# First gate computed by TensorE in units placed between attention's, with x modulated during the memory stage, more steps in each head, and the first feed-forward units split by K

## The reference, cut to what matters

```
mod = silu(c) @ w_ada + b_ada                 # one row of 2048 times 2048 x 12288
shift_m, scale_m, gate_m, shift_f, scale_f, gate_f = split(mod, 6)
h = rmsnorm(x) * (1 + scale_m) + shift_m
proj = h @ w_in                               # differential attention and MLA inputs
mix = concat(o_diff, o_mla) @ w_out
x = x + gate_m * mix
h = rmsnorm(x) * (1 + scale_f) + shift_f
x = x + gate_f * (relu(h @ w_ff1)**2 @ w_ff2)
# second block: memory keys and values from mem @ w_mem_kv, three attention branches,
# gates by sigmoid, output product
```

## Time and profile before

| | |
|---|---|
| median of 3 executions | 2192.8 us (2191.8 to 2196.15) |
| profiled execution, its own time | 2190.42 us |
| its span | 2188.6 us |
| mean granted TensorE clock | 0.961 of full speed |
| busy: PE, DVE, ACT, POOL | 2000.1, 1313.3, 945.3, 157.9 us |
| HBM read | 443 MB |

### The profile page before, as it was taken

The page is one execution under the profiler, slowest core; times in us unless marked ns, Lnnn a source line. Parts: engine busy times, 40 slices in busy tenths (PEclk is TensorE's granted clock), DMA queues, the critical chain, the costliest instruction groups (busy, mean ns, idle before and its releaser), DMA issues. The chain is left out here.

```text
span 2188.6 us, 24524 instructions
## 1 busy us (share of the span) xinstructions
PE 2000.1 (91%) x9240; PEld 1642.4 (75%) x9240; DVE 1313.3 (60%) x2057; ACT 945.3 (43%) x1440; POOL 157.9 (7%) x118
## 2 busy tenths in 40 slices
PE   6598897867789999999999999979999999999999
PEld 3276775546667888888888878878988877787877
DVE  3777876776796555555555555566555545545544
ACT  2453445343444344434434455445444444444433
POOL 0100000001000110110010021110100001101000
PEclk9798999878999999999999999989999999999999
DMA  9798775657797555555555555434534456656644
GB/s 356 284 327 307 244 250 199 235 189 278 290 340 255 192 192 184 192 193 186 188 193 187 187 193 179 149 100 126 164 108 149 126 169 198 192 182 187 194 170 170
DMA packets 128967, 448.82 MB, mean 205 GB/s; under 512 B 14288, under 2 KB 14544, under 8 KB 128336
## 3 DMA queue, kind: packets, MB, share of 16 engines
q1 hardware_dynamic: 124928, 433.74, 59.8%
q0 software_dynamic: 1568, 7.34, 0.9%
q10 hardware_dynamic: 2352, 6.17, 0.7%
HBM read 443.00 MB, written 4.19 MB: 204 GB/s over the span
## 5 line engine op out<-in xcount | busy, mean ns | idle before, releaser
L283 DVE TENSOR_TENSOR wlo<-raw,whi 128x1024 fp32r<-128x1024 f32 (+4 forms) x652 | 784.9, 1208 | 750.3 <-ACT whi L282 695.5
L282 ACT ACTIVATE whi<-raw 128x1024 fp32r<-128x1024 f32 (+4 forms) x652 | 658.3, 1012 | 836.6 <-PE g L397 707.0
L392 PE MATMUL g<-whi,lhsA_hi 128*128 128x512 f32 (+4 forms) x1840 | 715.8, 391 | 35.6 <-DVE lhsA_lo L788 28.0
L393 PE MATMUL g<-whi,lhsA_lo 128*128 128x512 f32 (+4 forms) x1840 | 698.0, 381 | 0.0
L397 PE MATMUL g<-wlo,lhsA_hi 128*128 128x512 f32 (+4 forms) x1840 | 470.0, 378 | 0.2 <-DVE wlo L283 0.2
L392 PEld LDWEIGHTS g<-whi,lhsA_hi 128*128 128x128 f32 x1840 | 357.3, 194 | 99.0 <-ACT tmp L780 21.8
L393 PEld LDWEIGHTS g<-whi,lhsA_lo 128*128 128x128 f32 x1840 | 357.6, 194 | 53.8 <-issue 1.4
L397 PEld LDWEIGHTS g<-wlo,lhsA_hi 128*128 128x128 f32 x1840 | 344.4, 193 | 56.2 <-DVE wlo L283 0.4
L537 DVE SCALAR_TENSOR_TENSOR raw<-raw,srow 128x1024 f32<-128x1024 f32 x181 | 217.5, 1224 | 17.8 <-DMA raw<-in_w_ada 17.5
L392 PE MATMUL g<-whi,lhsF_hi 128*128 128x512 f32 x512 | 200.6, 392 | 0.0
L393 PE MATMUL g<-whi,lhsF_lo 128*128 128x512 f32 x512 | 199.4, 389 | 0.0
(11 more groups left out here) (250 smaller groups left out, 1471.8 us busy)
## 6 DMA issues: line engine op xcount, KB each, us to landing
raw<-in_w_ff SPq DMA_DIRECT2D x256, 512.0 KB, 3.5
raw<-in_w_ada SPq DMA_DIRECT2D x181, 512.0 KB, 4.8
raw<-in_w_in SPq DMA_DIRECT2D x176, 512.0 KB, 4.2
raw<-in_w_out SPq DMA_DIRECT2D x64, 512.0 KB, 5.0
raw<-in_w_in SPq DMA_DIRECT2D x80, 384.0 KB, 3.1
raw<-in_w_branch_a SPq DMA_DIRECT2D x12, 512.0 KB, 3.5
raw<-in_w_branch_b SPq DMA_DIRECT2D x12, 512.0 KB, 4.3
raw_wide<-in_w_ada SPq DMA_DIRECT2D x11, 512.0 KB, 7.6
```

The lines of the kernel that those rows point to most:

```text
L282: t_hi = AC.put(lambda e: e.activation(hi, x, ACT.Copy), landed, free, us=0.2 + n * 0.00167)
L283: t_lo = DV.put(lambda e: e.tensor_tensor(lo, x, hi.bitcast(F32), ALU.subtract), landed, t_hi, free, us=0.15 + n * 0.00208)
L392: PE.put(lambda e, o=o, x=xh, w=h, f=first: e.matmul(o, x, w, start=f, stop=False), w, mark=False, us=us)
L393: PE.put(lambda e, o=o, x=xl, w=h: e.matmul(o, x, w, start=False, stop=False), mark=False, us=us)
```

## The change

**Gate.** The columns of gate_m leave `w_ada` and the deque (`adas` goes from 192 to 160 tiles) and become four native units `u_gate` of 8 tiles. silu(c) now also stands in a column form, `scol` (16 columns of 128). A matmul takes one column of it, repeated 128 times, as the stationary operand and 512 columns of the fp32 tile as the moving one: the product comes out as a row that is already spread over all partitions. A tile costs two fp32 matmuls (L374 of the changed kernel) and no work on ACT or DVE. The bias is loaded beforehand (`gate_bias`) and added when the product is read (`gate_rows`). The units stand at `("g", 0)` to `("g", 3)` in `order1`. `spread` remains for gate_f, with its diagonal blocks made on ACT.

**x early.** The norm of x and the modulation of x are in `bg` from the start of the memory stage; `mem_keys` comes after both memory units instead of between them, and `drain()` there is gone.

**More steps.** `diff_head`, `softmax_pv` (MLA and memory heads) and `causal_head` get one more `yield` before the transposes of the probabilities and one between the copy of the transposed probabilities and the product with the values. A copy of `diff_head` moves from DVE to ACT.

**Feed-forward.** Its first two units run their first K half (pairs 0 to 3) before the second one.

**Around it.** The dots of c = 20 to 23 may not start before the row norm `rr1`; `fill` steps over a slot that is taken instead of giving up; `g_final` is loaded after the norm instead of beside x.

```diff
@@ run
             ahead = j + (3 if plan[j][2] else 4)
-            while plan[j][2] and not plan[min(ahead, len(plan)) - 1][2]:
+            while state["ring"] > NRAW and not plan[min(ahead, len(plan)) - 1][2]:
                 ahead -= 1
             consume_to(ahead)
             pair = u["pairs"][i] + u["k_off"] // 2
+            if lhs is None:
+                slot, x, landed = halves[j]
+                for kk in range(2):
+                    o, sc = G[2 * par], scol[:, 2 * pair + kk:2 * pair + kk + 1].to_broadcast([P, P])
+                    waits = [landed, ready_c["scol"]] + (gfree[par] if i == kk == 0 else [])
+                    tok = PE.put(lambda e, o=o, sc=sc, w=x[:, kk * n:kk * n + n], f=i == kk == 0, z=i == 7 and kk == 1:
+                                 e.matmul(o[:, :], sc, w, start=f, stop=z), waits, mark=kk == 1, us=n * 0.00168)
+                raw_free[slot] = [tok]
+                pump(steps, width)
+                continue
@@ fill
-        while adas:
+        while adas and (adas[0][0] < 20 or "rr1" in t_of):
             i = state["slot"] % state["ring"]
             if raw_free[i] is None:
-                break
+                state["slot"] += 1
+                continue
@@ plan
-    order1 = (("h", 2), ("h", 3), ("l", 0), ("h", 0), ("l", 1), ("h", 4), ("l", 2), ("l", 3), ("h", 1), ("h", 5))
+    order1 = (("h", 2), ("h", 3), ("l", 0), ("h", 0), ("l", 1), ("h", 4), ("l", 2), ("g", 0), ("l", 3), ("h", 1), ("g", 1),
+              ("h", 5), ("g", 2), ("g", 3))
+        elif kind == "g":
+            u_gate[i], = mix([("w_gate", 512 * i, 512, 16, None)], native=True)
+        if g == 0:
+            u_f1 += mix([("w_ff1", 512 * i, 512, (0, 8), A_) for i in range(2)])
+            for u, v in zip(u_f1, mix([("w_ff1", 512 * i, 512, (8, 8), A_) for i in range(2)])):
+                u["tiles"], u["pairs"] = u["tiles"] + v["tiles"], list(range(8))
@@ gate
-    def spread(g, free):
+    def spread(free):
-                t = DV.put(lambda e, m=m, q=16 * g + 4 * j + m: e.tensor_scalar(rot[m], ident, gcols[:, q:q + 1], None,
-                                                                              ALU.mult), ada_done[c], t_cst, used_)
+                t = AC.put(lambda e, m=m, q=4 * j + m: e.activation(rot[m], ident, ACT.Copy, scale=gcols[:, q:q + 1]),
+                           ada_done[20 + j], t_cst, used_, us=0.3)
+    def gate_bias(h):
+
+        t_of["gate", h] = load(PO, gt[:, 1024 * h:1024 * h + 1024],
+                               a["b_ada"][0:1, 2 * D + 1024 * h:2 * D + 1024 * h + 1024].to_broadcast([P, 1024]), [DV.tok()])
+
+    def gate_rows(j):
+
+        par, tok = run(u_gate[j], width=4)
+        dst = gt[:, 512 * j:512 * j + 512]
+        gate_done[0, j] = DV.put(lambda e: e.tensor_tensor(dst, G[2 * par][:, :], dst, ALU.add), tok, t_of["gate", j // 2],
+                                 us=0.6)
+        gfree[par] = [gate_done[0, j]]
@@ memory stage
     for j in range(8):
         bg.append(mem_turned(j))
     bg.append(row_norms(ms, t_m, ssm, rm, "rm"))
+    bg.append(row_norms(xs, t_x, ssx, rx, "rx"))
+    for j in range(8):
+        bg.append(modulated(j, [xs[:, t, (2 * j + i) * P:(2 * j + i + 1) * P] for i in range(2) for t in range(2)],
+                            lambda j=j: t_of["xs", j // 2], 0))
...
     par, tok = run(u_mem[0], width=3, adas_per_pair=2)
-    drain()
+    while "rm" not in t_of:
+        pump(1, 3)
     r = take(rows)
     ks = evac2(par, tok, 512, r.ap, t_of["rm"], r.free, scale=(rm[:, 0:1], rm[:, 1:2]))
-    bg.append(mem_keys(r, ks))
-    bg.append(row_norms(xs, t_x, ssx, rx, "rx"))
-    angles()
-    lam()
-    par, tok = run(u_mem[1], adas_per_pair=2)
+    par, tok = run(u_mem[1], width=3, adas_per_pair=2)
     t_of["mv"] = evac2(par, tok, 512, mv, t_of["rm"], scale=(rm[:, 0:1], rm[:, 1:2]))
     narrow()
+    angles()
+    lam()
     while ("xs", 3) not in t_of:
-        pump()
+        pump(1, 3)
+    bg.append(mem_keys(r, ks))
@@ diff_head, softmax_pv, causal_head (each)
+        yield
         T = yield from grab(TB)
...
         T.release([k])
+        yield
         O = yield from grab(OB)
@@ feed-forward
+    t_of["gfin"] = load(PO, gfin, a["g_final"].rearrange("(a d) -> a d", a=1).to_broadcast([P, D]), fence)
+        if g == 0:
+            for u in u_f1[0:2]:
+                run(u, width=3, hi_i=4)
         for i in range(4):
-            par, tok = run(u_f1[4 * g + i], width=3)
+            par, tok = run(u_f1[4 * g + i], width=3, lo_i=4 * (g == 0 and i < 2))
```

More of the change, by code:

```diff
@@ L261, in fetch @@
     def fetch(src, n):
+        while raw_free[state["slot"] % state["ring"]] is None:
+            state["slot"] += 1
         i = state["slot"] % state["ring"]
@@ L401, in run @@
         u["tok"] = tok
-        lhs.free = [tok]
+        if lhs is not None:
+            lhs.free = [tok]
         return par, tok
@@ L570, in build @@
     gate_done = {}
-    def spread(g, free):
+    def spread(free):
         used_ = [PE.tok()]
         for j in range(4):
-            c = 8 + 12 * g + j
-            wanted["gate"] = [c]
-            while c not in ada_done:
+            wanted["gate"] = [20 + j]
+            while 20 + j not in ada_done:
                 yield
             for m in range(4):
-                t = DV.put(lambda e, m=m, q=16 * g + 4 * j + m: e.tensor_scalar(rot[m], ident, gcols[:, q:q + 1], None,
-                                                                              ALU.mult), ada_done[c], t_cst, used_)
+                t = AC.put(lambda e, m=m, q=4 * j + m: e.activation(rot[m], ident, ACT.Copy, scale=gcols[:, q:q + 1]),
+                           ada_done[20 + j], t_cst, used_, us=0.3)
             yield
@@ L617, in build @@
                                                               op0=ALU.add, op1=ALU.mult), k1)
+    scol = sm(16)
+    kc = AC.put(lambda e: e.activation(scol, vec[:, V_C:V_C + 16], ACT.Tanh, scale=0.5), k)
+    kc = DV.put(lambda e: e.scalar_tensor_tensor(out=scol, in0=scol, scalar=1.0, in1=vec[:, V_C:V_C + 16], op0=ALU.add,
+                                                 op1=ALU.mult), kc)
+    ready_c["scol"] = DV.put(lambda e: e.tensor_scalar(scol, scol, 0.5, None, ALU.mult), kc)
     k = DV.put(lambda e: e.tensor_scalar(vec[:, V_SUB:V_SUB + 1], vec[:, V_SUB:V_SUB + 1], 1.0 - LAM0, None,
@@ L708, in mem_turned, with modulated @@
                    [t_vec])
+    def modulated(j, src, src_tok, sec, ready=None):
+        cs = [4 * sec + (sec // 2) * 4 + j // 2, 4 * sec + (sec // 2) * 4 + 4 + j // 2]
+        wanted[j] = cs
+        while any(c not in ada_done for c in cs) or (sec == 0 and ("xs", j // 2) not in t_of):
+            yield
+        b = yield from grab(SOB)
+        tok = turn_rows(b, src, src_tok())
+        yield
+        tm = yield from grab(tmps)
+        for i in range(2):
+            kk = 2 * j + i
+            gcol, scol = mods[:, 16 * (sec + 1) + kk:][:, 0:1], mods[:, 16 * sec + kk:][:, 0:1]
+            tt = AC.put(lambda e, i=i, g=gcol, s=scol: e.activation(
+                tm.ap[:, 256 * i:256 * i + 256], b.ap[:, 256 * i:256 * i + 256], ACT.Identity, bias=s, scale=g),
+                tok, tm.free, [ada_done[c] for c in cs])
+        b.release([tt])
+        hi = lhsA.hi[:, 2 * j:2 * j + 2, :].rearrange("p a b -> p (a b)")
+        lo = lhsA.lo[:, 2 * j:2 * j + 2, :].rearrange("p a b -> p (a b)")
+        th = AC.put(lambda e: e.activation(hi, tm.ap[:, :], ACT.Copy), tt, lhsA.free)
+        yield
+        tl = DV.put(lambda e: e.tensor_tensor(lo, tm.ap[:, :], hi.bitcast(F32), ALU.subtract), th, lhsA.free)
+        tm.release([tl])
+        lhsA.ready[j] = tl
     for j in range(8):
@@ L740, in mem_keys @@
         yield from heads_norm(r, 4, 128, tok)
+        for _ in range(4):
+            yield
         for j in range(2):
@@ L1121, in build @@
                         bg.append(diff_head(h))
+        elif kind == "g":
+            gate_rows(i)
         else:
@@ L1134, in build @@
     lhsA.ready[4:8] = [None] * 4
-    bg.append(spread(0, gate_free))
     bg.append(diff_end(0))
@@ L1149, in reload @@
         x_tok.extend([t_xr] for _ in range(4))
-        t_of["gfin"] = load(PO, gfin, a["g_final"].rearrange("(a d) -> a d", a=1).to_broadcast([P, D]), w)
     bg.append(reload())
```

78 lines of the change are left out of this document (31 added, 47 removed).

## The result

| | before | changed |
|---|---|---|
| median of 5 runs each | 2192.3 us | 2208.3 us |
| ratio, 95% interval | | 1.007 [1.0053, 1.0087] |
| profiled execution: time, span | 2190.4, 2188.6 us | 2208.95, 2207.2 us |

The change made the kernel slower by 16 us, and the forecast was faster by 16. Three marks in TensorE's timeline divide the span: the first matmul on pair 6 (208.90 us before), the first transpose of the feed-forward (592.38 us), the end. The first stretch ends at 209.52 us instead of 208.90; the middle takes 404.6 us instead of 383.5; the last 1593.1 instead of 1596.2. Together +18.6, the difference of the spans. The middle as cut here ends with the wait for the rows' norm, which fell from 10.76 to 8.09 us. Up to that wait the stretch takes 396.5 us (209.5 to 606.0) where it took 372.7: 23.8 us more.

A forecast was written before the change was run, and what follows sets the result against it. Before 700 us it saw DMA bounding 98 to 209 us, then PE waiting for the heads' chains with nothing saturated; -13 + 5 - 1 - 1 - 6 = -16 gave 2177 us, range 2152 to 2195.

The forecast's parts named there:

- The memory stage, -13: Up to pair 6: keys taken out and x put between tiles start w_in loads sooner; -13 us, between -3 and -20.
- Three tiles more (10.5) and about 3.6 us of transposes end at 80.4 us: Memory stage: PE's end after the keys' wait goes, so the first w_in load could issue at 81, 16.6 us sooner.
- Rival 3: Before 209 us: late loads and the 5-slot ring make DMA idle, first term falls to -3, 2187 us; chance 0.10.
- The middle stretch, +5: 209 to 582 us: gate work +51.8, idle -65.2 with 27 left, clock -13, loads +4; bounds -26 and +31.
- clock's credit of 13: Middle stretch: 13 us credited for a faster PE clock, bounds 0 and 25.
- Left 7 + 17 = 24; I take 27: Middle stretch: PE idle time left of 65.2 us, latents' 7 plus 17 beside the last heads, taken as 27.
- 45 left and 5 of clock give +27: Middle stretch: upper bound with 45 us of idle time left and 5 of clock credit; +31 with the loads.
- The loads' +4: Last two gate units: SP issues loads slower than PE uses them, 0.4 us for each of 16 tiles, partly hidden.
- Rival 2: Middle stretch: gate tiles too short a cover for head steps, stretch +27, whole +6, 2199 us; chance 0.12.
- Rival 1: Middle stretch: gate tiles fill nearly all waits, stretch -26, whole 2146 us, half way 2160; chance 0.20 with half way.
- Feed-forward's start, -1 and -1: K halves save only smaller waits, -1 (0 to -5); dots of c = 20 to 23 behind the norm, -1.
- The second block, -6: The added yields remove waits of pO (4.3, 2.6 and 2.6 us) in the second block's heads; -6 us (0 to -12).

The follow-up runs named there:

- e11: Changed kernel with x's first two pairs turned behind the last memory tile and the angles ahead of the second memory unit: 2196.5 us, 1.0026 of before.
- e13: e8 plus the changed memory stage, x's first two pairs turned behind the last memory tile, angles earlier; gate stays dots: 2175.2 us, 0.9933 of before.
- e2: Kernel before with only the added steps in the heads of both blocks and the heads' copy on ScalarE: 2189.4 us, 0.9989 of before.
- e9: Changed kernel with two listed steps, not four, taken forward behind each gate tile: 2214.9 us, 1.0109 of before.
- e10: Changed kernel with the fourth gate unit and its loads moved behind the first output-projection unit: 2211.7 us, 1.0092 of before.
- e1: Changed kernel with the first gate again as dots on VectorE and spread by fp32 matmuls: 2191.5 us, 0.9998 of before.
- e7: Changed kernel with each gate matmul over the first 64 of 512 columns, loads and order unchanged: 2191.8 us, 1.001 of before.
- e4: Changed kernel with one of the two matmuls of each gate tile left out, loads and order unchanged: 2194.3 us, 1.0016 of before.
- e12: e8 plus the feed-forward begun by K halves: 2186.1 us, 0.9975 of before.
- e8: Kernel before with only the two added steps of the second block's causal heads: 2186.1 us, 0.9977 of before.

## Why the prediction was wrong

**The memory stage, -13: it was 0, and most of it could be had.** The step that failed is "Three tiles more (10.5) and about 3.6 us of transposes end at 80.4 us". It gave the transposes their own time and no wait for what they read. Dots on VectorE stand ahead of x's norm, so they waited 11.39 us with five memory tiles behind them, and the load queue stood still for 16 us (61.88 to 77.87). The first load of `w_in` went out at 92.72 us where 81 was forecast; in e11 it goes out at 84.26. The step also counted one tile too few: four memory tiles stand behind the 13.19 us wait in the kernel before (16 matmuls behind the keys' first transposes in TensorE's order, 4 to a tile), not three, so its own sum ends at 84. Rival 3 came near in size (-3), for a reason that decided less: the middle of the stage kept the gain. Its batch of 12 loads took 14.40 us, 6.9 more than the seven, where 5.4 was charged. The size of the term was high but of the right order: e11 has -9.4 at pair 6 against before, e13 -7.5. That DMA passes the gain on held too.

**The middle stretch, +5: it was +24 up to the norm's wait.** The gate's price was right: 10 matmuls (20 records) in 8.75 us, 0.875 us each, one repeated column as stationary operand at the plain price. In the prediction's terms the stretch was +51.8 of work, -64.8 of idle time, +45.1 left and -8.3 of clock (TensorE is busy for 351.4 us where it was 307.9, which is 43.5 more, not 51.8). So the clock's credit of 13 was 5 too high. What failed is "Left 7 + 17 = 24; I take 27": 45 were left. The forecast waits went, but others came. I counted waits as places and emptied them by name, while e2, e9 and e10 show that a wait for a head's chain can move instead of going. VectorE's 39 us were to count "only through what waits for DVE"; between e1 and e7 no gain from them shows. The upper bound of that term, "45 left and 5 of clock give +27", held it. The loads' +4 were not seen in the changed kernel, where TensorE waited 0.2 us for `w_gate`; with less matmul beside them, in e4 and e7, they were (3.6 and 3.8 us of waits).

Rival 2 was the right sign, and its bound of about 48 us of idle time left is close to the 45 measured. Its mechanism, a cover too short behind each step, is there in part: some 13 us of idle time stand behind gate tiles, where it asked for 22 more than forecast, and they grow as the tiles get shorter (e4, e7). It is not the whole: the time fell in e4 and e7 all the same, and in e9, where the tiles are the same length and better spread, it rose. What is shown is that the gate on TensorE costs 15.8 us (e1) and that taking half of it away gives 11.8 back. Why e9 is slower is not shown.

**Rival 1** leaned on a rule of the Trainium skill (TensorE: Matmul & The Clock Gate, "Loop structure matters more than you think"). This case agrees in kind, with 0.86 granted in e7 and 0.93 in the changed kernel over 394 us, and e4's scores at 1.22 us behind a wait; the time still rose: the clock gave 8.3 us and the idle time 20, against 51.8 us of added work.

**Feed-forward's start, -1 and -1:** the wait was 8.09 instead of 10.76 us, the 4.46 stayed; e12 shows no gain by the halves. The wait is 8.1 us in every kernel with the gate's units and 9.97 to 14.27 in every one with dots, e1 among them (10.53), which has the halves and the late `g_final`; so it goes with the gate and not with these two. The dots behind the norm were not tried by themselves.

**The second block, -6:** -4.5 by medians, 3 to 7 by the interval, for the causal heads' steps alone (e8). Right. New is that the same edit gains nothing in the first block without gate tiles and 14 us beside them; the prediction had no term for that coupling.

**The sum.** By the marks of the two profiles it was +0.6 for the memory stage, +23.8 for the middle, -2.7 for the norm's wait and -3.1 for all behind it, together +18.6. Two terms went wrong in one direction, by 14 and 19 us. The range reached to the loss of one of them at a time. The edits' own prices do not add: the steps of the first block gained nothing without the gate and 14 us beside it.

## What to carry to other kernels

When work is moved into an ordered queue ahead of other work, ask when its operands are ready before asking how long it takes; a stall is worth what stands behind it, here the loads of five tiles. Work put onto the bounding engine to fill its waits can be cheap for the first part only: measure half of it before all, and look whether its loads alone set a floor. And do not count on time back from relieving an engine that is not saturated, as VectorE here, without a run that shows it.

## What the runs showed of the hardware

A matmul whose stationary operand is one column repeated 128 times costs the same as a plain one, 0.875 against 0.88 us for 128x512 fp32. A gate tile took 1.88 us at the granted full clock and 3.78 at half of it (0.50 granted), twice as long, and the tile that ends a wait may be the slow one while the rows behind it are fast again (364.65, then 368.23 us above). The middle stretch of the six kernels with the same order of TensorE's work there differed by up to 8 us between single executions (399.3 to 407.6), with different stages ahead of it; most of the edits are worth less.
